# Strassen block products for 23 of 28 dense weight slots per layer of a hybrid decoder step

## What is computed

```python
z = h @ p["w_in"][l]                       # 1024 x 10240
u, v, q, k, vr, gr, ga, gb = jnp.split(z, ...)
u = jax.nn.gelu(u)
v = layernorm(jax.nn.gelu(v), ...)
a = chunk_spatial_gating(u, v, w_s, b_s)
q = rotary(q, pos);  k = rotary(k, pos) * (R_QK_DIM ** -0.5)
y, r_new = retention(q, k, vr, r0, chunk)
b = jax.nn.silu(gr) * head_groupnorm(y)
merged = jax.nn.sigmoid(ga) * (a @ w_a_out) + jax.nn.sigmoid(gb) * (b @ w_b_out)
x = x + gt1 * (merged @ w_o)
x = x + gt2 * hier_moe(rmsnorm(x) * (1 + sc2) + sh2)   # top-1 of 4 groups, top-2 of 8 experts
```

## Time and profile before

| | us |
|---|---|
| median of 3 runs | 1699.34 (1697.1, 1699.34, 1702.22) |
| span of the profiled execution, first to last instruction | 1698.6 |
| TensorE matmul busy | 1655.2 (97%) |
| VectorE busy | 525.8 (31%) |
| ScalarE busy | 257.9 (15%) |

### The profile page before, as it was taken

One profiled execution on the slowest core, in us unless ns is written; L12 is line 12 of the kernel. 1 busy time (PEld: TensorE's weight loads), 2 busy tenths in 40 slices (PEclk: granted clock), 3 DMA queues, 4 the chain that ended last, 5 costly groups with the idle time before them and its releaser, 6 DMA issues.

```text
span 1698.6 us, 20215 instructions
## 1 busy us (share of the span) xinstructions
PE 1655.2 (97%) x8224; PEld 952.8 (56%) x8224; DVE 525.8 (31%) x1291; ACT 257.9 (15%) x510; POOL 46.3 (3%) x93
## 2 busy tenths in 40 slices
PE   6999999999999999999999999999999999999997
PEld 2677764445577654444447776554547765444443
DVE  1220220223611354443442213102253126343336
ACT  3110001101210331111131100010112013211111
POOL 0000000000100000000000000000010010000000
PEclk9999999999999999999999999999999999999999
DMA  9633656558943659999983336543887443999993
GB/s 398 241 127 117 235 211 235 211 216 322 407 189 140 237 190 414 421 422 420 422 349 123 112 140 235 211 147 113 330 363 310 149 151 136 358 419 420 421 421 151
DMA packets 47022, 451.68 MB, mean 266 GB/s; under 512 B 5633, under 2 KB 5889, under 8 KB 7505
## 3 DMA queue, kind: packets, MB, share of 16 engines
q1 hardware_dynamic: 43200, 409.66, 60.4%
q10 hardware_dynamic: 3456, 37.75, 5.3%
q0 software_dynamic: 272, 2.97, 0.4%
HBM read 411.16 MB, written 39.19 MB: 265 GB/s over the span
## 4 chain that ended last, share of the span: by engine, by line
PE 78%; issue 15%; DMA 3%; DVE 2%; POOL 1%; ACT 1%; DVEq 0%; POOLq 0%; SPq 0%; ACTq 0%
PE ps L672 78%; DMA prm<-params 2%; ACT work L1064 1%; POOL rstd L593 0%; DMA cst<-consts 0%; POOL kzm L625 0%; DVEq L1296 0%; POOLq L592 0%; DVE hT L1800 0%; DVE work L1637 0%; DVE work L1634 0%; POOL prm L604 0%; DVE rope L1351 0%; DVE work L1744 0%; ACT prm L1064 0%
## 5 line engine op out<-in xcount | busy, mean ns | idle before, releaser
L672 PE MATMUL ps<-ring,work 128*64 128x512 f32 x1536 | 338.7, 595 | 2.7 <-ACT work L1064 2.7
L672 PE MATMUL ps<-ring,hT 128*32 128x128 f32 (+1 forms) x1920 | 318.2, 382 | 2.4 <-ACT hT L1064 2.4
L672 PE MATMUL ps<-hT,ring 128*128 128x288 f32 x1280 | 317.5, 410 | 1.9 <-DVE work L1637 1.9
L672 PEld LDWEIGHTS ps<-hT,ring 128*128 128x128 f32 x1280 | 244.3, 192 | 72.9 <-issue 6.1
L672 PE MATMUL ps<-work,ring 128*128 128x288 f32 x1024 | 249.6, 406 | 4.2 <-issue 2.3
L672 PEld LDWEIGHTS ps<-ring,hT 128*32 128x32 f32 (+1 forms) x1920 | 154.3, 137 | 167.9 <-issue 163.2
L1064 ACT ACTIVATE work<-ps 128x512 f32<-128x512 f32 (+5 forms) x244 | 109.5, 467 | 829.5 <-PE ps L672 828.7
L672 PEld LDWEIGHTS ps<-ring,work 128*64 128x64 f32 x1536 | 114.0, 137 | 209.8 <-issue 206.1
L672 PEld LDWEIGHTS ps<-work,ring 128*128 128x128 f32 x1024 | 194.2, 190 | 58.8 <-issue 5.5
L672 PE MATMUL ps<-work 128*128 128x288 f32 (+7 forms) x800 | 191.2, 401 | 4.7 <-DVE hT L1774 2.6
L672 PEld LDWEIGHTS ps<-work 128*128 128x128 f32 (+2 forms) x800 | 126.7, 186 | 68.0 <-issue 33.2
(11 more groups left out here) (178 smaller groups left out, 798.5 us busy)
## 6 DMA issues: line engine op xcount, KB each, us to landing
ring<-stream SPq DMA_DIRECT2D x96, 2048.0 KB, 8.8
ring<-stream SPq DMA_DIRECT2D x192, 1024.0 KB, 10.4
state_sample_out<-ring ACTq DMA_DIRECT2D x16, 2048.0 KB, 8.7
state_out<-prm ACTq DMA_DIRECT2D x8, 512.0 KB, 9.1
prm<-params SPq DMA_DIRECT2D x1, 2608.5 KB, 24.7
prm<-params POOLq DMA_DIRECT2D x1, 2608.5 KB, 16.3
cst<-consts SPq DMA_DIRECT2D x1, 1651.0 KB, 17.4
xT<-x_in SPq DMA_DIRECT2D x1, 1152.0 KB, 7.2
```

The lines of the kernel that those rows point to most:

```text
L672: return nc.tensor.matmul(out, lhsT, rhs, start=start, stop=stop, **k)
```

## The change

Each of 23 slots per layer (v,1; u; ga; a; q; k; vr; gr; b,1 to b,3) is computed with Strassen's scheme in the variant with common sums. Activations and weights are cut into 2 x 2 blocks; seven block products take the place of eight. The token blocks are tokens 128 to 287 ("RIGHT", 160 wide, the 32 samples ride along) and tokens 0 to 127 ("LEFT"). Sums of activation blocks are made once for three sets of activations (`token_sums`). Sums of weight blocks are made by VectorE, in place in the ring, for every slot (`turn_weights`), and the results are put together by VectorE (`join`). v,0, gb, b,0 and o stay as they are.

```diff
+RIDE = P + NS
+SEVEN_KINDS = ("u", "ga", "a", "q", "k", "vr", "gr")
+SEVEN_TILES = ["m1", "m3", "c11", "m5", "m6", "m7", "m4"]
+def seven(step):
+    kind, i = step
+    return kind in SEVEN_KINDS or kind in ("v", "b") and i >= 1
...
+            if _t == "c11":
+                use((_l, _s, _t), TILES[_l, _s, "m1"][0])
+                continue
...
+            def feature_seven(l, step, act, sums, sums_n):
...
+                def product(name, tokens, kh, nh, fresh=True):
+                    part = part_of(w, kh, nh)
+                    wait_free(pe, (l, step, name))
+                    out, width = out_of(l, step, name), tokens.shape[2]
+                    for c in range(part.shape[2] // P):
+                        for k in range(half):
+                            last = mm(out[:, c, 0:width], part[:, k, c * P:c * P + P], tokens[:, k, :],
+                                      fresh and c == 0 and k == 0, k == half - 1, skip_group_check=True)
+                    made(last, (l, step, name))
+
+                product("m1", act[:, 0:half, RIGHT], 0, 0)
+                pe.wait_ge(sums_ready, 3 * l + sums_n)
+                product("m3", s4, 1, 1)
+                product("c11", act[:, half:2 * half, RIGHT], 1, 0, False)
+                pe.wait_ge(weights_ready, 4 * n + 1)
+                product("m5", s1, 0, 1)
+                pe.wait_ge(weights_ready, 4 * n + 2)
+                product("m6", s2, 1, 1)
+                pe.wait_ge(weights_ready, 4 * n + 3)
+                product("m7", s3, 0, 0)
+                pe.wait_ge(weights_ready, 4 * n + 4)
+                product("m4", act[:, half:2 * half, LEFT], 1, 0)
```

`token_seven` is the same with the tokens stationary: after the sample tile "s" as before, each product is 4 calls of 256 columns. On ScalarE and VectorE:

```diff
+            def first_partial(l, step):
+                key, n = (l, step, "m1"), SEVEN_AT[l, step]
+                wait_made(act, key)
+                if n > 0:
+                    before = list(SEVEN_AT)[n - 1]
+                    wait_reads(act, [(*before, "m7")])
+                taken(apply(partial(step)[0], out_of(l, step, "m1"), ACT.Copy), key)
+            def bend(l, step, parts, func):
+                c11, c12, c22, c21 = parts
+                wait_made(act, (l, step, "c11"))
+                taken(apply(c11, out_of(l, step, "c11"), func), (l, step, "c11"))
+                wait_reads(act, [(l, step, "m3")])
+                apply(c12, c12, func)
+                wait_reads(act, [(l, step, "m5")])
+                apply(c22, c22, func)
+                wait_reads(act, [(l, step, "m4")])
+                apply(c21, c21, func).then_inc(bent, 1)
...
+            def token_sums(act, sums):
...
+                dve.tensor_tensor(s1[:, :, 0:P], a21, a22, ALU.add)
+                dve.tensor_tensor(s3, a11[:, :, 0:P], a21, ALU.subtract)
+                dve.tensor_copy(s1[:, :, P:RIDE], a11[:, :, P:RIDE])
+                dve.tensor_copy(s4[:, :, P:RIDE], a12[:, :, P:RIDE])
+                settle()
+                dve.tensor_tensor(s2, s1[:, :, 0:P], a11[:, :, 0:P], ALU.subtract)
+                settle()
+                dve.tensor_tensor(s4[:, :, 0:P], a12[:, :, 0:P], s2, ALU.subtract).then_inc(sums_ready, 1)
+            def turn_weights(l, step):
+                n = LOAD_AT[l, step]
+                dve.wait_ge(slot_loaded[n % RING], 16 * (n // RING + 1))
...
+                if step[0] in ("v", "vr", "gr"):
+                    wait_made(dve, (l, step, "s"))
+                dve.tensor_tensor(b12, b12, b11, ALU.subtract).then_inc(weights_ready, 1)
+                settle()
+                wait_made(dve, (l, step, "m3"))
+                dve.tensor_tensor(b22, b22, b12, ALU.subtract).then_inc(weights_ready, 1)
+                settle()
+                dve.tensor_tensor(b11, b22, b11, ALU.subtract).then_inc(weights_ready, 1)
+                wait_made(dve, (l, step, "c11"))
+                dve.tensor_tensor(b21, b21, b22, ALU.subtract).then_inc(weights_ready, 1)
+            def join(l, step, c12, c22, c21):
+                first, upper, lower = partial(step)
+                wait_reads(dve, [(l, step, "m1")])
+                wait_made(dve, (l, step, "m6"))
+                taken(dve.tensor_tensor(first[:, :, 0:P], first[:, :, 0:P], out_of(l, step, "m6")[:, :, 0:P], ALU.add), (l, step, "m6"))
+                settle()
+                wait_made(dve, (l, step, "m5"))
+                dve.tensor_tensor(upper, first, out_of(l, step, "m5"), ALU.add)
+                wait_made(dve, (l, step, "m7"))
+                taken(dve.tensor_tensor(lower, first[:, :, 0:P], out_of(l, step, "m7")[:, :, 0:P], ALU.add), (l, step, "m7"))
+                settle()
+                taken(dve.tensor_tensor(c12, upper, out_of(l, step, "m3"), ALU.add), (l, step, "m3"))
+                taken(dve.tensor_tensor(c22, lower, out_of(l, step, "m5")[:, :, 0:P], ALU.add), (l, step, "m5"))
+                wait_made(dve, (l, step, "m4"))
+                taken(dve.tensor_tensor(c21, lower, out_of(l, step, "m4")[:, :, 0:P], ALU.add), (l, step, "m4"))
...
+                    elif kind == "u":
+                        turn_weights(l, step)
+                        join(l, step, *parts_of(step)[1:])
+                    elif kind == "ga":
+                        if i == 1:
+                            token_sums(uT, sums_u)
+                        turn_weights(l, step)
+                        join(l, step, *parts_of(step)[1:])
...
                     elif step == ("v", 1):
+                        turn_weights(l, step)
+                        join(l, step, *parts_of(step)[1:])
                         dve.wait_ge(rest_loaded, 32)
                         dve.wait_ge(params_loaded[l], 16)
                         for tt in range(2):
                             settle()
-                            wait_reads(dve, [(l, ("v", s), f"p{tt}") for s in range(2)])
+                            wait_reads(dve, [(l, ("v", 0), f"p{tt}")])
+                            dve.wait_ge(bent, BENT_AT[l, step] + 1)
                             moments_of([vn[:, tt, 0:512], vn[:, tt, 512:1024]], tt, l)
```

More of the change, by code:

```diff
@@ L829, in _ @@
                     elif kind == "kts":
-                        out = wait_free(pe, (l, step, "t"), [(l, (m, s), f"c{c}") for m in "qk" for s in range(2) for c in range(4)])
+                        pe.wait_ge(turned_ready, 4 * l + 4)
+                        out = wait_free(pe, (l, step, "t"))
                         for dt in range(2):
@@ L1648, in _ @@
                     elif kind == "a":
-                        for c in range(4):
-                            out = wait_made(dve, (l, step, f"c{c}"))
-                            at = merged[:, 4 * i + c, :]
-                            if i == 0 and c == 0:
-                                wait_reads(dve, [(l, ("ga", s), f"c{cc}") for s in range(2) for cc in range(4)])
-                            taken(dve.tensor_tensor(at, at, out[:, 0:TOK], ALU.mult), (l, step, f"c{c}"))
+                        turn_weights(l, step)
@@ new lines, in _ @@
+                        gates, sums = parts_of(step), quarters(step)
+                        if i == 0:
+                            dve.wait_ge(bent, BENT_AT[l, ("ga", 1)] + 1)
+                        wait_made(dve, (l, step, "c11"))
+                        taken(dve.tensor_tensor(gates[0], gates[0], out_of(l, step, "c11"), ALU.mult), (l, step, "c11"))
+                        join(l, step, *sums)
+                        settle()
+                        for n in range(3):
+                            dve.tensor_tensor(gates[1 + n], gates[1 + n], sums[n], ALU.mult)
@@ new lines, in _ @@
+                        wait_made(dve, (l, step, "c11"))
+                        taken(rotate(dst, 2 * i, RIGHT, out_of(l, step, "c11")), (l, step, "c11"))
+                        c12, c22, c21 = quarters(step)
+                        join(l, step, c12, c22, c21)
+                        settle()
+                        rotate(dst, 2 * i + 1, RIGHT, c12)
+                        rotate(dst, 2 * i + 1, LEFT, c22)
+                        rotate(dst, 2 * i, LEFT, c21)
+                        dve.nop().then_inc(turned_ready, 1)
```

217 lines of the change are left out of this document (177 added, 40 removed).

## The result

The changed kernel takes 1655.75 us (median of 4 runs, 1654.22 to 1657.38) against 1698.46 us for the kernel before in the same comparison: ratio 0.9748, 95% interval 0.9734 to 0.9761. The forecast was 1652.4 us, range 1640 to 1678. The span of the profiled execution is 1655.8 us, 42.8 less than before; the sum had said 46.9 less. One execution of a later experiment (ga with eight products) took 7329.77 us and is used nowhere.

What follows compares the result with a forecast made beforehand. The prediction took TensorE's streamed columns to set the pace outside the expert pairs, with room on VectorE. Its terms, -67.1 + 13.8 + 3.4 + 0.6 + 2.4 = -46.9, gave 1652.4 us, range 1640 to 1678.

Steps and rivals of the forecast that it cites:

- Columns: In 26 feature slots and 18 token slots, fewer streamed columns save 1.41 and 1.69 us a slot, together -67.1 us.
- The slower rival, short records in long streams: In the 26 feature slots, short records with own weight loads cost 0.025 us more each: +73, 1725 us; chance 0.05.
- Stall in u,0: TensorE waits for u,0's first weight sum, queued behind VectorE's normalisation: 7.0 and 6.5 us, +13.8 with latencies.
- Clock: Behind each u,0 stall TensorE's clock falls to half rate, costing 1.7 us each time, +3.4 us.
- the prediction's own sign of being wrong: Wrong if PE showed gaps in every slot, 160-column records stood at 0.15, or the expert pairs' time changed at all.
- ga,0: At ga,0 the first weight sum comes late, after VectorE's mixing work: +0.3 us a layer, +0.6 in the sum.
- o: Ahead of o, TensorE's gap behind the last piece of b,3 grows from 1.13 to 2.3 us: +1.2 a layer.
- q and k: In q and k slots, the tightest ones, VectorE's weight sums stay hidden under products with 1.6 us to spare.
- Queues: No load is added; stored states leave 1.0 us later through ScalarE, costing nothing, at worst 0.2 us.
- PSUM: Six or seven tiles a slot still meet seven banks; the longest-waiting, m3's, is taken some 9 us before its bank's turn.

Runs made afterwards that it cites:

- ga with eight products: Changed kernel with both ga slots of each layer computed as before the change, with eight products; 1657.99 us, ratio 0.9762 to the kernel before.
- u by eight: Changed kernel with both u slots of each layer computed as before the change, with eight products; 1637.53 us, ratio 0.9641 to the kernel before.
- two and six more in q and k: Changed kernel with two or six unread VectorE statistics instructions added behind the rotations of each q and k slot; 1657.15 us with two, 1681.21 us with six.
- the first experiment: Changed kernel with u,0's weight sums moved ahead on VectorE, the first before v,1's moments, three before the normalisation; 1639.79 us, ratio 0.9651.
- split normalisation: Changed kernel with u,0's weight sums moved ahead of the normalisation and the second token tile normalised after u,0 is joined; 1636.05 us, ratio 0.964.

## Why the prediction was right, point by point

**Columns.** -67.1 forecast, about -65.4 measured, with both halves off. A feature slot fell by 1.47 (17.96 to 16.49 for k,0 with its mod slot), forecast 1.41; the 160-column record stands at 0.136 (0.137 taken, bounds 0.134 to 0.140). A token slot, gr,0 in layer one, fell from 331.01 - 315.30 = 15.71 to 315.76 - 301.69 = 14.07, by 1.64 (1.69), but others by less: vr,0 with its mod slot from 17.93 to 16.61, by 1.32, and gr,1 with the state behind it from 19.81 to 18.30, by 1.51. So 26 x 1.47 = 38.2 instead of 36.7, and the 18 token slots make 27.2 instead of 30.4 (the vr slots 5.3 in layer one and 6.3 in layer two, six gr slots at 1.51, the gr,0 and v,1 slots at 1.64, which for v,1 is taken over from gr,0). The slower rival, short records in long streams, is refuted: the 112 records of k,0 take 212.94 - 198.79 = 14.15 us, 0.126 each, as expected, and not 0.139 or more. The rule of the Trainium skill (TensorE: Matmul & The Clock Gate, "Back-to-back issue gap"), that in streams of pairs of load and product one of 128 columns takes 25 ns more than alone, does not show in this kernel's float32: its records stand at 0.112 with 128 columns and 0.136 with 160, close to the line to 0.242 with 288.

**Stall in u,0.** Forecast 7.0 and 6.5, measured 6.44 and 6.44. Its cause, place and releaser are the forecast ones; moving the sums in the queue removed it.

**Clock.** Forecast +3.4 for the two stretches behind the stall, measured 1.6 and 1.9. What failed is the step that placed no other cost on the clock, and with it the prediction's own sign of being wrong: "I'd be wrong if ... the pairs' time changed at all". It did. The stage from the router on grew by 2.3 us in each layer. 1.5 and 1.7 of this are the slow stretch in the second pair's row (12.22 us in both layers, where the kernel before had 10.73 and 10.52). The rest differs: in layer one +0.4 in routing and +0.4 behind the second pair's row, in layer two +1.7 in routing (a wait of 1.69 us for ScalarE where before there was none) and -1.2 behind that row. In layer one's routing one slow stretch fell away against waits of the same size, as PE alone shows before and then after:

```profile
593.58 3.47 PE L672 MATMUL ps<-ring,cT 128*32 128x512 f32 x16
...
570.22 1.92 PE L758 MATMUL ps<-ring,cT 128*32 128x512 f32 x16
...
573.57 5.80 PE L758 MATMUL ps<-work 128*128 128x352 f32 x24 [0.84 <-DVE work L1636]
```

This growth is no steady price of the seven products. Five experiments that keep all or most of them have the second pair's row at 10.52 in both layers (sums first, u by eight, ga by eight, two and six more in q and k), and their stages from the router on take 291.3 to 292.9 and 295.4 to 296.9 us, near the 292.0 and 295.4 of the kernel before. What decides where such a stretch falls stays open.

**ga,0.** +0.3 a layer forecast, 0.3 found by leaving out the sums. **o.** The gap grew from 1.13 to 2.03, +0.9 a layer instead of 1.2. **q and k.** Hidden with 1.85 to spare, forecast 1.6; shown by adding work. **Queues.** No wait for weights or states appeared in gr and st. **PSUM.** No wait in the changed kernel, as forecast, but the margin was 3.0 to 7.1 us and not some 9, and the first experiment used it up.

So -67.1 + 13.8 + 3.4 + 0.6 + 2.4 = -46.9 became, measured, about -65.4 + 12.9 + 3.5 + 0.6 + 1.8 + 4.6 = -42.0, and the trace says -42.8; the last 0.8 is not placed. The largest miss, 4.6 us, is the stage that the prediction put at nothing; its range had allowed 3.4 more for the clock, but only behind the stall. The median was forecast 3.4 us low and not 4.1, because the kernel before had its median at 1698.46 in this comparison and not at 1699.34. Also, the profiled execution isn't one of the three times given before: in every run on record the span lies 1.5 to 1.6 us under its own time, so the span of 1698.6 belongs to a time near 1700.15, and the 0.7 between span and median was no property of the kernel. No term changed its sign.

## What to carry to other kernels

Price a change in a matmul's shape by the pitch of its records (starts, not mean durations), and an added helper engine's work by its place in that engine's queue: some 200 us of weight sums cost almost nothing in 42 slots, and the sums of the one slot a layer behind a long normalisation cost 16. When such a sum stalls, move it ahead of the long job, but then look at what the long job now delays; here the tiles that waited to be joined held PSUM banks. Read experiments by stages: the clock's slow stretches add or take some 2 to 8 us of the total in places that the edit doesn't touch, enough to hide the 5 us that seven products in u are worth.

## What the runs showed of the hardware that I had not expected

The total time at half clock was not a constant of the kernel. The same wait of 0.95 us ahead of ga,0 was followed by a slow product (3.3 to 4.1 us for 16 records) in 8 of 20 rows in the kept traces of ten kernels and not in the other 12 (2.41). The mean granted clock ran from 0.987 (changed kernel) to 0.995 (split normalisation), that is, twice 0.013 or 0.005 of the span, about 43 or 16 us, was at half rate (an estimate from those means). Behind the wait of 6.4 us in u,0 the clock was slow each time the wait stood empty and full both times it was filled with products. For the waits of about 1 us no such link is shown: the stretch behind them came and went from one program to the next without being filled. So a comparison of two programs can differ by some microseconds for this alone.
